# Two hand-overs between stages cut into token halves

## The reference

```
mod = silu(c) @ ada_w + ada_b            # shifts, scales, gates: columns of 1024
y = swiglu_ffn(h, w_ffn_in, w_ffn_out)   # or the mixer with its output product w_o
x = x + g * (rms_norm(y) * post_g)       # norm over the 1024 features of a token
h = rms_norm(x) * pre_g * (1 + sc) + sh  # the next stage's input, a norm of the new x
z = h @ w_next                           # the next stage's first product
```

## Time and profile before

| | us |
|---|---|
| median of 3 runs | 1404.26 |
| profiled execution, its own time | 1405.93 |
| its span | 1404.1 |
| PE busy | 1342.2 (96%) |
| DVE busy | 823.6 (59%) |
| ACT busy | 588.5 (42%) |
| POOL busy | 407.2 (29%) |
| PE waiting for the spread's reciprocal, line 336 | 5.9 in 7 spreads |

### The profile page before, as it was taken

The page is one execution under the profiler, slowest core; times in us unless marked ns, Lnnn a source line. Parts: engine busy times, 40 slices in busy tenths (PEclk is TensorE's granted clock), DMA queues, the critical chain, the costliest instruction groups (busy, mean ns, idle before and its releaser), DMA issues. The chain is left out here.

```text
span 1404.1 us, 19406 instructions
## 1 busy us (share of the span) xinstructions
PE 1342.2 (96%) x7840; PEld 1068.1 (76%) x7840; DVE 823.6 (59%) x966; ACT 588.5 (42%) x849; POOL 407.2 (29%) x191
## 2 busy tenths in 40 slices
PE   5999999889999999999999999999999999999996
PEld 3778867668888888887778886777786799777775
DVE  2789974476655654323766665777842842566644
ACT  4323646333222222112454347867732422455551
POOL 0000000039988888999100000000000050233310
PEclk9999999979999999999799999999999899999998
DMA  9434052215454445554132334333322342111121
GB/s 385 145 146 150 31 208 96 87 34 204 171 219 179 179 179 183 210 180 185 51 130 84 104 115 121 113 113 102 117 90 91 123 169 89 70 50 42 61 91 60
DMA packets 41350, 181.12 MB, mean 129 GB/s; under 512 B 3392, under 2 KB 20160, under 8 KB 21312
## 3 DMA queue, kind: packets, MB, share of 16 engines
q1 hardware_dynamic: 40128, 171.73, 33.9%
q10 hardware_dynamic: 1152, 8.39, 1.8%
HBM read 173.75 MB, written 6.36 MB: 128 GB/s over the span
## 5 line engine op out<-in xcount | busy, mean ns | idle before, releaser
L193 DVE TENSOR_TENSOR wlo<-raw,whi 128x2048 fp32r<-128x2048 f32 x95 | 257.1, 2707 | 172.0 <-ACT whi L189 169.4
L200 POOL TENSOR_TENSOR ada_raw<-ada_raw,cs 128x2048 f32<-128x2048 f32 x36 | 144.6, 4018 | 495.2 <-DVE h2lo L454 446.9
L271 PE MATMUL ps<-hhi,whi 128*128 128x512 f32 x640 | 252.0, 394 | 2.4 <-PEq L566 0.8
L271 PE MATMUL ps<-hhi,wlo 128*128 128x512 f32 x640 | 249.4, 390 | 0.0
L271 PE MATMUL ps<-hlo,whi 128*128 128x512 f32 x640 | 249.1, 389 | 0.0
L189 ACT ACTIVATE whi<-raw 128x2048 fp32r<-128x2048 f32 x95 | 181.6, 1911 | 141.7 <-PE ps L1315 91.3
L209 POOL TENSOR_TENSOR ada_raw<-ada_raw 128x1024 f32<-128x1024 f32 x72 | 166.0, 2305 | 5.6
L271 PEld LDWEIGHTS ps<-hhi,whi 128*128 128x128 f32 x640 | 120.2, 188 | 28.7 <-issue 2.4
L271 PEld LDWEIGHTS ps<-hhi,wlo 128*128 128x128 f32 x640 | 120.1, 188 | 25.6
L271 PEld LDWEIGHTS ps<-hlo,whi 128*128 128x128 f32 x640 | 120.3, 188 | 24.4
L2054 POOL TENSOR_TENSOR x<-x,rest 128x256 f32<-128x256 f32 (+3 forms) x32 | 49.1, 1533 | 153.2 <-DVE rest L2349 153.2
(11 more groups left out here) (374 smaller groups left out, 2760.6 us busy)
## 6 DMA issues: line engine op xcount, KB each, us to landing
raw<-panels SPq DMA_DIRECT2D x87, 1024.0 KB, 4.9
ada_raw<-ada SPq DMA_DIRECT2D x48, 1024.0 KB, 6.7
first<-ada SPq DMA_DIRECT2D x8, 1024.0 KB, 20.2
bc<-ac_rows SPq DMA_DIRECT2D x32, 256.0 KB, 3.7
raw<-panels ACTq DMA_DIRECT2D x8, 1024.0 KB, 5.0
x_kept<-x SPq DMA_DIRECT2D x2, 2048.0 KB, 9.5
x<-x_kept SPq DMA_DIRECT2D x2, 2048.0 KB, 8.3
x<-x_in SPq DMA_DIRECT2D x1, 2048.0 KB, 10.3
```

The lines of the kernel that those rows point to most:

```text
L193: e.tensor_tensor(wlo[:, c % 2, :, :], raw[:, c % 2, :, :], whi[:, c % 2, :, :].bitcast(F32), ALU.subtract).then_inc(lo_split, 1)
L200: e.tensor_tensor(ada_raw[:, c % 2, :, :], ada_raw[:, c % 2, :, :], cs[:, which, :].unsqueeze(2).to_broadcast([P, KT, 256]), ALU.mult).the ...
L271: mm = e.matmul(ps[:, 2 * (qc % 2) + b, :], w[:, c % 2, 2 * k + b, :], src[part][:, k, :], **flags)
```

## The change

`post_norm` gives way to one function, `boundary`, which makes the post-norm, the new x, the pre-norm and the next stage's first panel by halves of 256 tokens; `pre_norm` stays for the other places. Only the first two banks of the last panel are still written whole.

```diff
+        TILES = [7, 6, 5, 4, 0, 1, 2, 3]
+        PAIRS = (3, 2, 0, 1)
+        HALF = (slice(0, S // 2), slice(S // 2, S))
+        ROWS = (slice(0, P // 2), slice(P // 2, P))
+        def boundary(post, gate, gain, sc, sh, y, sq, last, late):
...
+            def half_sums(pe, a, bank, src, first, final):
+                for i in range(2):
+                    b = 2 * a + i
+                    mm = pe.matmul(ps[32 * b:32 * b + 32, bank, 0:P], ones[:, 0:32], src[:, i * P:(i + 1) * P], ...
+            def half_spread(pe, n, a, bank):
+                pe.wait_ge(*no("rs_ready", n + 1))
+                for b in (2 * a, 2 * a + 1):
+                    mm = pe.matmul(ps[:, bank, b * P:(b + 1) * P],
+                                   ident[ROWS[a], 32 * b:32 * b + 1].to_broadcast([P // 2, P]), rsq[ROWS[a], :], ...
...
+            def on_pe(pe, part, c, qc):
+                for j in range(2):
+                    part(TILES[j], slice(0, S)).then_inc(N["bank_done"], 1)
+                for j in range(2, KT):
+                    part(TILES[j], HALF[0]).then_inc(N["bank_done"], 1)
+                    if j == 5:
+                        for t in range(4):
+                            sums(pe, 0, t)
+                for j in range(2, KT):
+                    pe.wait_ge(*no("kept", j + 1))
+                    part(TILES[j], HALF[1]).then_inc(N["bank_done"] if j < KT - 1 else panels_used, 1)
+                    if j == 2:
+                        for t in range(4, KT):
+                            sums(pe, 0, t)
+                    if j == 4:
+                        half_spread(pe, 0, 0, 7)
+                    if j == 6:
+                        for t in range(6):
+                            sums(pe, 1, t)
+                for t in (6, 7):
+                    sums(pe, 1, t)
+                columns(pe, 0)
+                for r in range(4):
+                    sums2(pe, 0, r)
+                half_spread(pe, 1, 1, 6)
+                columns(pe, 1)
+                half_spread(pe, 2, 0, 5)
...
+                for a in range(2):
+                    for k in range(KT):
+                        for half, weights in ((0, (whi, wlo)), (1, (whi,))):
+                            pe.wait_ge(*no("lo_ready" if half else "hi_ready", a * KT + k + 1))
+                            for b in range(2):
+                                for w in weights:
+                                    mm = pe.matmul(ps[:, 2 * (qc % 2) + b, HALF[a]], w[:, c % 2, 2 * k + b, :],
+                                                   (hhi, hlo)[half][:, k, HALF[a]], ...
+                        if (a, k) == (0, 5):
+                            for r in range(4):
+                                sums2(pe, 1, r)
+                    if a == 0:
+                        columns(pe, 2)
+                        half_spread(pe, 3, 1, 7)
...
+            def on_act(act):
...
+                std(0, 7, 8)
+                for j in range(2, KT - 1):
+                    square(1, j, HALF[1])
+                    keep(j)
+                square2(0, 1)
+                square2(0, 0)
+                square(1, 7, HALF[1])
+                square2(0, 3)
+                std(1, 6, 8)
+                square2(0, 2)
+                std(0, 5, 12)
+                keep(7)
+                for k in range(KT):
+                    high(0, k)
+                    if k in (1, 3, 4, 5):
+                        square2(1, (1, 3, 4, 5).index(k))
+                    if k == 6:
+                        std(1, 7, 12)
+                split_part(0)
+                split_part(1)
+                for k in range(KT):
+                    high(1, k)
+                    if k in (1, 3):
+                        split_part(2 + k // 2)
...
+            def on_dve(dve):
...
+                for j in range(2):
+                    keep(j, slice(0, S))
+                split_lo(dve, last + 1, 0)
+                for j in range(2, KT):
+                    keep(j, HALF[0])
+                recip(0, 0)
...
+                scale(0, 0, both(y, 0, 0))
+                for i, bank, count in ((1, 5, 1), (3, 0, 3)):
+                    room = ps[:, bank, :].rearrange("p (h s) -> p h s", h=2)
+                    if i == 3:
+                        scale(0, 2, both(y, 2, 0))
+                    dve.wait_ge(*no("kept_b", count))
+                    scale(0, i, room)
+                    add(0, i, room)
+                recip(1, 1)
+                recip(2, 0)
+                dve.wait_ge(*no("spread", 2))
+                scale(1, 0, both(y, 0, 1))
+                dve.wait_ge(*no("spread", 3))
...
+                for k in range(KT):
+                    norm(0, k)
+                    if k < 3:
+                        dve.wait_ge(*no("kept_b", 2 * k + 2))
+                        scale(1, k + 1, both(y, k + 1, 1))
+                    if k == 3:
+                        add(1, 3, both(y, 3, 1))
+                low(0, KT - 1)
+                recip(3, 1)
+                for q in range(2):
+                    split_part(q)
+                dve.wait_ge(*no("spread", 4))
...
+                for k in range(KT):
+                    norm(1, k)
+                low(1, KT - 1)
+                for q in range(2, 4):
+                    split_part(q)
+                dve.wait_ge(*no("lo_parts", 4))
+                dve.sem_inc(lo_split, 1)
+            X_NEW0 = [(0, 0), (0, 2), (1, 0), (1, 1), (1, 2)]
+            def on_pool(pool):
+                for a, i in X_NEW0:
+                    pool.wait_ge(*no("scaled", 4 * a + i + 1))
+                    pool.tensor_tensor(both(x, i, a), both(x, i, a), both(y, i, a), ALU.add) ...
...
-                post1["pe"](pe, lambda b: [out_part(3, b, k2) for k2 in range(2)][1])
-                pre1["pe"](pe, w0 + 4, 10)
+                step1["pe"](pe, lambda b, cols: [out_part(3, b, k2, cols) for k2 in range(2)][1], w0 + 4, 10)
...
-                post2 = post_norm("ffn_post", "g2", ..., last, late=(41, 54, sums, [3, 3, 1, 1, 2, 3]))
+                step2 = boundary("ffn_post", "g2", ..., last, late=(41, 54, sums, [4, 4, 5]))
```

More of the change, by code:

```diff
@@ L371, in post_norm, with sums @@
-            a0, a1, sums, parts = late or (0, 0, None, [0] * 6)
+            def half_sums(pe, a, bank, src, first, final):
+                for i in range(2):
+                    b = 2 * a + i
+                    mm = pe.matmul(ps[32 * b:32 * b + 32, bank, 0:P], ones[:, 0:32], src[:, i * P:(i + 1) * P], start=first,
+                                   stop=final, skip_group_check=True)
+                return mm
+            def sums(pe, a, j):
+                if j == 0:
+                    pe.wait_ge(*no("kept", a + 1))
+                pe.wait_ge(*no("sq_ready", j + 1 if j < 2 or a == 0 else j + 7))
+                half_sums(pe, a, 7 - a, place(a, j), j == 0, j == KT - 1).then_inc(N[sums_of[a]], 1)
@@ new lines, in scale, with add, low @@
+                def scale(a, i, place):
+                    dve.tensor_tensor(place, both(y, i, a), ps[:, 7 - a, HALF[a]].unsqueeze(1).to_broadcast([P, 2, S // 2]),
+                                      ALU.mult).then_inc(N["scaled"], 1)
+                def add(a, i, place):
+                    dve.wait_ge(*no("scaled", 4 * a + i + 1))
+                    dve.tensor_tensor(both(x, i, a), both(x, i, a), place, ALU.add).then_inc(N["x_new1"], 1)
+                def low(a, k):
+                    n = a * KT + k
+                    dve.wait_ge(*no("hi_ready", n + 1))
+                    dve.scalar_tensor_tensor(out=hlo[:, k, HALF[a]], in0=h0(n), scalar=m(sh)[:, k:k + 1],
+                                             in1=hhi[:, k, HALF[a]].bitcast(F32), op0=ALU.add,
+                                             op1=ALU.subtract).then_inc(N["lo_ready"], 1)
@@ new lines, in norm @@
+                def norm(a, k):
+                    n = a * KT + k
+                    if n >= 4:
+                        dve.wait_ge(*no("lo_ready", n - 3))
+                    dve.scalar_tensor_tensor(out=h0(n), in0=x[:, k, HALF[a]], scalar=coef[:, 1, k:k + 1],
+                                             in1=ps[:, (5, 7)[a], HALF[a]], op0=ALU.mult,
+                                             op1=ALU.mult).then_inc(N["h0_ready"], 1)
+                    if k >= 1:
+                        low(a, k - 1)
@@ new lines, in split_part @@
+                def split_part(q):
+                    cp = last + 2
+                    dve.wait_ge(*no("hi_parts", q + 1))
+                    tiles = slice(4 * q, 4 * q + 4)
+                    ins = dve.tensor_tensor(wlo[:, cp % 2, tiles, :], raw[:, cp % 2, tiles, :],
+                                            whi[:, cp % 2, tiles, :].bitcast(F32), ALU.subtract)
+                    ins.then_inc(N["lo_parts"], 1)
+                for j in range(2):
+                    keep(j, slice(0, S))
@@ L1333, in _ @@
                         pe.wait_ge(lo_split, last + 1)
[L1334 to L1335 removed]
```

(2 more changed lines are left out.)

215 lines of the change are left out of this document (122 added, 93 removed).

## The result

The changed kernel took 1418.11 us (median of 4 runs, 1414.59 to 1420.87); the kernel before, measured beside it, took 1403.24 us (1401.50 to 1405.87). The ratio is 1.0103, with a 95% interval of 1.0074 to 1.0132: some 15 us slower. The forecast of 1406.3 us missed, and so did its range, whose end was 1413.0.

What follows compares the result with a forecast made beforehand. TensorE is 96% busy; the hand-overs lose time to a chain hopping between engines. First hand-over 43.4 us (-2.6), second 50.2 (+3.1), behind it +1.5: +2.0 us, 1406.3 us, range 1396.5 to 1413.

Steps and rivals of the forecast that it cites:

- one sign of being wrong: In the stretch from the first normalisation on: VectorE idle over 4 us would show the forecast wrong.
- (a): First hand-over, TensorE's panel by halves: matmuls 11.4 us, sum records 2.0, half spread 1.5; last matmul near t = 15.
- (b): First hand-over, first half's chain of keeps, sums, root, reciprocal, spread and scales: first normalisation at t = 20.2, not 30.5.
- (c): After the first normalisation VectorE bounds: 0.39 us per 256-column operation, 6.2 us per token half, four reciprocals of 0.95.
- (d) The lock: GpSimd's adds for the second half's x beside VectorE's low parts, locking a shared port: 1.5 us, ends 0 and 2.5.
- (d) The second detour: ScalarE's high part 7 waits behind the second half's root: with the other wait, 2.0 us of idle VectorE (0.5 to 4).
- (f): End of a hand-over: low split is VectorE's last work, panel load waits for it, then programs change: 1.2 us.
- rival B: TensorE at 1.2 GHz bounds the half panels: 4 us more per hand-over, +10.0 with detours, 1414.3 us; chance 0.15.
- Second hand-over over the first: Columns +1.7, +2.0 and +1.5, low split +1.1, more stretches at 1.2 GHz +0.5: 6.8 us over 43.4, giving 50.2.
- Behind it: After the second hand-over, a panel load just ahead of the small load delays it: 1.5 us lost (0 to 2.2).
- A: Rival: overlap works as drawn, no locks, detour 0.5; hand-overs 40.4 and 45.1 us, 1396.7 in all; chance 0.20.
- C: Rival: columns, locks and small load at their upper ends: +8.6 us, 1412.9; chance 0.12.

Runs made afterwards that it cites:

- e3: The changed kernel with GpSimd's three additions of the second half of x left out in both hand-overs; ratio 1.0061.
- e11: e8 with ScalarE taking the first half's last tile and first split part before the second half's root, VectorE a split part before the reciprocal; ratio 1.0009.
- e8: The changed kernel with the small load before the panel's, columns moved out of the chain and extra matmuls in TensorE's waits; ratio 1.0038.
- e6: The changed kernel with the matmuls of the second hand-over's 13 late columns left out; second hand-over 49.0 us.
- e7: The changed kernel with the old functions in the second hand-over, so the change in the first alone; 1405.37 us, ratio 1.0030.
- e2: The changed kernel with the second hand-over's 13 late columns moved out of TensorE's chain to later places; ratio 1.0089.
- e12: The changed kernel run again, nothing edited; 1418.72 us, ratio 1.0120.
- e4: The changed kernel with 20 extra matmuls into a free PSUM bank in TensorE's waits in each hand-over; 1417.24 us, ratio 1.0104.

## Why the prediction was wrong

The sign of the point was right, and that was partly luck: the first hand-over was to win 2.6 us and lost 1.8. Forecast was +2.0 us in all; 16.1 are found from the first hand-over on in the profiled pair (12.7 in the spans, 3.4 of chance ahead of it). The steps that failed are the sum of 43.4 us for a hand-over, which measured 47.8 (and carried its 4.4 us of error into the second one, 55.3 against 50.2), and the 1.5 us for what is behind, which measured 5.7. The signs that the prediction named mostly came true: the first normalisation at 21.2 and 27.7 us, the long low parts, the late small load. So did one sign of being wrong: at the second hand-over VectorE was idle for 5.3 us from its first normalisation on. By its own steps:

- **(a) and (b), the way to the first normalisation: t = 20.2, measured 21.2.** The lost microsecond is the term "the 56 sum records at the rate of 24 in 0.86 us". They go at 24 in 1.50 us. The step took the duration of a record over from a form in which four matmuls in a row cover four token blocks, to one in which two do. The panel's last matmul starts at t = 16.1, where 15 was laid out.
- **(c) VectorE's operations: right.** 0.39 us each from start to start, four reciprocals of 0.95, as charged.
- **(d) The lock: right.** 1.34 and 1.32 us for two low parts are 1.7 us more than alone, 1.5 charged; e3 shows the cause.
- **(d) The second detour: mis-sized.** 2.0 us of idle VectorE charged, 3.21 and 3.51 measured in the first trace, and never under 2.48 in another with this order. Half cold spacing for the 256-column matmul, 0.213 us, was right to the digit, but the sums behind part 5 take 1.94 us, which is the first error again. e11 shows what the detour was worth: 1.4 us at the first hand-over, 1.5 at the second.
- **(f) Second half, split parts and change of program: 8.8 us charged, 10.4 measured** (292.67 to 303.12). VectorE needs 8.37 to 8.39 us of it in every trace of the new order, against 7.6 charged. It ended at 301.05, TensorE at 302.47: at the lower clock TensorE was the bound of the second half panel. Where the clock was kept there, TensorE ended 0.6 us before VectorE, and the change of program took the 1.2 us that were charged and not 2.07. I had named this as rival B, with its condition "the clock still low at the fourth part of each half", and given it 0.15 because the earlier trace rows show the clock back within the first panel. In this trace the condition came true in both halves. Its price was 1.6 us at the first hand-over, not 4 (47.8 against 46.2 in e8 with the clock held): VectorE and TensorE bind the half panels almost equally. In e6 and e7 the clock was low in the first half alone, and that cost nothing inside the hand-over (46.2). At the second, with columns between the tiles, e8 is 4.4 us under e2, though other edits lie between them, so this part stays open.
- **First hand-over in all:** 43.4 charged, 47.8 measured. Up to the first normalisation +1.0; from there to the last reciprocal, with operations, locks and detour, +1.8 (14.0 us against 12.2); from it to the second half 0.0; over the second half and its split parts +0.8; behind them +0.9, which is the lower clock. No single term failed; four stretches all failed the same way.
- **Second hand-over over the first: +6.8 charged, +7.5 and +7.2 measured.** As a sum the terms were good. Apart they were less so: e6 puts the columns at 4.8 to 6.3 us (5.2 charged) and the rest at 2.8 (1.6 charged). Sums at 1.2 GHz, for which the sum had only 0.5 us of "more stretches at 1.2 GHz", added 1.6 in one of two traces. The forecast of 50.2 failed by the base of 43.4 that it was added to.
- **Behind it: +1.5 charged, +5.7 measured** (2.9 as a wait, 2.8 as clock; 4.1 in e12). The mechanism was named, its place and its rows were right. Its size failed twice: 0 to 2.2 us for the small load, when it was 2.9, because I let the load ahead of it land after its usual 4.9 us, when it took 5.7 with others behind it on the queue, and the small one landed only after it (713.87 and 714.36); and nothing at all for what a wait in a full TensorE does to its clock. This was the costliest term left at nothing, and the earlier trace rows had shown the clock going down in the waits of both hand-overs.
- **The range** came from cases with one cause each. A, B and C were priced apart and added by chance, not by size; what happened was part of B and part of C together, with a third cause behind them.

## What to carry to other kernels

When a hand-over is split to let engines overlap, first ask what its waits were doing: here they hid 13 groups of columns, the split of a panel and GpSimd's additions, and in the new order each of these cost more. Take the fixed cost of every form from a row of that form, and treat every new wait on TensorE as two costs, the wait and the clock after it. And try the cheap cure first: where TensorE waits on others in a chain, extra matmuls into a free bank kept this kernel's clock at 2.4 GHz through most of both hand-overs and made the old order 6.2 us faster (0.9956), more than any form of the new one.

## What the runs showed of the hardware that I had not expected

- Sums with 32 output columns took 0.036 us a record when four matmuls in a row went to four different groups of output partitions, and 0.063 to 0.069 us when they used two groups in turn (24 in 0.86 and in 1.50 us). In the first form four records start within 0.02 us and the next four 0.11 us later; in the second it is two and two. No run isolates this.
- VectorE waited 1.92 to 2.12 us, in eight traces, for a load of 32 columns when it stood first on the queue, and 4.67 to 6.23 us in the six traces in which a 1 MB load had gone out 0.8 to 1.5 us earlier. In each of the six the small load landed 0.3 to 0.5 us after the large one.
- The clock fell to 0.50 for some 3 us within a dense panel, 0.1 to 0.7 us after its start, in five traces of the new order. It had been at 1.00 for 17 us or more before, and in e4 TensorE's longest idle stretch of the whole hand-over was the 1.8 us just ahead of that panel.
- VectorE's low split of 2048 columns took 2.28 us alone, and beside GpSimd's reductions at the second hand-over between 2.89 and 5.27 us in the fourteen traces, with no edit there.
